# One fused Mamba-2 scan product per token tile for both directions, in a one-core Trainium2 kernel

## The reference

```python
dt = jax.nn.softplus(dt + dt_bias)             # per token, direction and head (32 heads of 64 columns)
yc_f, hc_f = ssd_chunked(x_c, dt_c[:, :, 0], a[0], b_c, c_c, h0)      # forward, context, then latent from its state
yc_b, hc_b = ssd_chunked(flip(x_c), flip(dt_c[:, :, 1]), a[1], flip(b_c), flip(c_c), h0)     # backward
...
y = (yf + flip(yb)).astype(xs.dtype) + xs * d_skip[:, None]
y = y.reshape(bb, ll, SSD_D_INNER) * jax.nn.silu(z)                    # then a norm per group, then @ w_out
```

## Time and profile before

| | |
|---|---|
| median of three runs | 1770.62 us |
| the profiled execution's own time | 1770.7 us |
| its span in the trace | 1768.9 us |
| mean granted TensorE clock | 0.979 of full |
| PE, DVE, ACT, POOL busy, share of the span | 89%, 35%, 21%, 14% |
| the scan: first and last of line 943's matmuls start | 276.3 and 490.1 us |

### The profile page before, as it was taken

The page is one execution under the profiler, slowest core; times in us unless marked ns, Lnnn a source line. Parts: engine busy times, 40 slices in busy tenths (PEclk is TensorE's granted clock), DMA queues, the critical chain, the costliest instruction groups (busy, mean ns, idle before and its releaser), DMA issues. The chain is left out here.

```text
span 1768.9 us, 22244 instructions
## 1 busy us (share of the span) xinstructions
PE 1582.5 (89%) x8812; PEld 832.7 (47%) x8812; DVE 613.4 (35%) x1294; ACT 370.6 (21%) x761; POOL 253.2 (14%) x266
## 2 busy tenths in 40 slices
PE   5999999999999979899788788798989998878887
PEld 3534445666545555455444344344555544444443
DVE  2433447778724223422111112647422211111112
ACT  2221146887710110000000000217210000000000
POOL 2001013434320010110101012111011110101001
PEclk9899999999999989999999999899989999999999
DMA  9477767999260489999999999822479999999996
GB/s 376 176 283 299 288 229 185 317 319 309 72 254 24 155 336 426 425 425 425 426 428 426 428 427 417 340 111 75 185 274 424 425 425 426 426 427 427 426 426 259
DMA packets 141922, 572.77 MB, mean 324 GB/s; under 512 B 22360, under 2 KB 79208, under 8 KB 111120
## 3 DMA queue, kind: packets, MB, share of 16 engines
q1 hardware_dynamic: 121296, 525.49, 74.2%
q0 software_dynamic: 14784, 26.11, 4.1%
q10 hardware_dynamic: 5760, 20.06, 3.5%
HBM read 543.52 MB, written 49.25 MB: 335 GB/s over the span
## 5 line engine op out<-in xcount | busy, mean ns | idle before, releaser
L1944 PE MATMUL bank<-mem 128*64 128x256 f32 x4160 | 503.1, 393 | 73.3 <-DMA mem<-in_moe_w_gate_dram 45.3
L1944 PEld LDWEIGHTS bank<-mem 128*64 128x64 f32 x4160 | 296.4, 136 | 279.2 <-issue 50.3
L1957 PE MATMUL bank<-mem 128*64 128x512 f32 x1040 | 238.3, 600 | 44.0 <-DMA mem<-in_moe_w_down_dram 38.7
L626 PE MATMUL bank<-mem 128*128 128x512 f32 x384 | 173.3, 604 | 0.9 <-DMA mem<-in_ssd_w_in_dram 0.9
L1890 POOL DMA_INDIRECT ys_dram<-mem x61 | 61.2, 1003 | 771.1 <-DVE mem L2178 700.1
L2108 ACT ACTIVATE mem<-bank 128x256 f32<-128x256 f32 x65 | 24.9, 383 | 685.0 <-PE bank L1944 685.0
L1957 PEld LDWEIGHTS bank<-mem 128*64 128x64 f32 x1040 | 70.8, 137 | 172.3 <-issue 117.2
L2178 DVE TENSOR_TENSOR mem<-bank,mem 128x512 f32<-128x512 f32 x65 | 44.9, 691 | 222.1 <-PE bank L1957 167.2
L2157 DVE TENSOR_TENSOR mem<-mem,bank 128x256 f32<-128x256 f32 x65 | 27.4, 421 | 268.3 <-PE bank L1944 135.2
L626 PEld LDWEIGHTS bank<-mem 128*128 128x128 f32 x384 | 71.9, 192 | 99.4 <-issue 97.6
L920 PE MATMUL bank<-mem 128*128 128x512 f32 x256 | 115.2, 593 | 0.0
(11 more groups left out here) (333 smaller groups left out, 1505.4 us busy)
## 6 DMA issues: line engine op xcount, KB each, us to landing
mem<-in_moe_w_up_dram SPq DMA_DIRECT2D x64, 2048.0 KB, 26.4
mem<-in_moe_w_down_dram SPq DMA_DIRECT2D x64, 2048.0 KB, 26.7
mem<-in_moe_w_gate_dram SPq DMA_DIRECT2D x63, 2048.0 KB, 26.4
mem<-in_mod_w_dram SPq DMA_DIRECT2D x24, 2048.0 KB, 9.0
ys_dram<-consts SPq DMA_DIRECT2D x55, 512.0 KB, 7.8
mem<-in_ssd_w_in_dram SPq DMA_DIRECT2D x10, 2048.0 KB, 9.3
mem<-ac_dram ACTq DMA_DIRECT2D x32, 512.0 KB, 5.6
mem<-in_ssd_w_out_dram SPq DMA_DIRECT2D x4, 2048.0 KB, 11.0
```

The costliest lines, as they stand in the source:

```text
L626: mm = nc.tensor.matmul(psum[c % 2][:, :], lhsT=w[:, k, (c % 4) * P:(c % 4 + 1) * P], rhs=aT[0][:, k, :], start=(k == 0), stop=(k == KD - 1))
L1944: mm = nc.tensor.matmul(bank[half * BR:(half + 1) * BR, 0:HF], lhsT=x[:, k], rhs=w[k][:, half::2], start=(k == 0), stop=(k == KD - 1), ski ...
L1957: mm = nc.tensor.matmul(bank[half * BR:(half + 1) * BR, :], lhsT=ht[:, k // 2, k % 2 * BR:(k % 2 + 1) * BR], rhs=w[:, k, half * COLS:(half ...
```

## The change

It does five things. dt goes out of the product: after the decays, `lndt` = ln(max(dt, 1.2e-38)) is formed (one DVE, one ACT instruction), `ltop` is its largest value over the heads, and the column term `acol` gets ltop − lndt added (three DVE instructions); the Exp of each piece gets a bias from `ltop`, so it yields decay·dt. The `xdt` multiply on POOL goes, and line 943's product reads x itself. The decay matrices are made per tile, forward then backward (`piece`, tiles 3, 2, 1, 0), in three buffers `EB`. In each odd step POOL adds the two masked matrices of a tile (128x1024), and only then PE multiplies the sum by x: eight products in odd steps, none in even ones. And DVE's tail changes: an odd step evacuates bank 5, a step from place 2 on bank 6, 16 adds instead of 20 per group.

The diff, with waits and helpers of the later stages left out:

```diff
@@ -705,6 +705,9 @@
...
         nega = region(A_WORK + 5760, 64)
+        lndt = tmp6[3]
+        ltop = small(2 * NT)
+        DT_TINY = 1.2e-38
         dtrow = region(A_Y + 2048, 512)
...
@@ -759,6 +762,7 @@
...
                                     bc(nega.rearrange("p (d h) -> p d h", d=2), 1, NT), ALU.mult).then_inc(dt_A, 1)
+            nc.vector.tensor_scalar(lndt, dtf, DT_TINY, None, ALU.max).then_inc(dt_w, 1)
         def decay_dve(dve):
...
@@ -768,6 +772,12 @@
...
                 nc.vector.tensor_tensor(wend[:, d], EX[:, d, :, 1, :], dt[:, :, d, :], ALU.mult).then_inc(wend_ok, 1)
+            dve.wait_ge(dt_l, 2)
+            ln = lndt.rearrange("p (t d h) -> p t d h", t=NT, d=2)
+            link(dve, nc.vector.tensor_reduce(ltop, lndt.rearrange("p (n h) -> p n h", h=HEADS), AX, ALU.max))
+            link(dve, nc.vector.tensor_tensor(ln, bc(ltop.rearrange("p (t d) -> p t d", t=NT), 3, HEADS), ln,
+                                              ALU.subtract))
+            nc.vector.tensor_tensor(acol, acol, ln.rearrange("p t d h -> p d t h"), ALU.add).then_inc(wend_ok, 1)
         def dt_act(act):
...
@@ -785,6 +795,8 @@
...
                                      ACT.Exp).then_inc(ex_ev, 1)
+            act.wait_ge(dt_w, 2)
+            nc.scalar.activation(lndt, lndt, ACT.Ln).then_inc(dt_l, 1)
         def decay_pe(pe):
...
@@ -803,13 +815,12 @@
...
         y = region(A_WORK, 4096, "p (b t n) -> p b t n", b=2, t=NT)
-        xdt = region(A_WORK + 4096, 1024, "p (b r n) -> p b r n", b=2, r=HG)
         xw = region(A_WORK + 5120, 1024, "p (b r n) -> p b r n", b=2, r=HG)
...
         acB = region(A_Y + 2048, 2048, "p (b r n) -> p b r n", b=2, r=HG)
-        EB = region(A_Y + 4096, 2048, "p (b r n) -> p b r n", b=2, r=HG)
+        EB = [region(at, 1024, "p (r n) -> p r n", r=HG) for at in (A_Y + 4096, A_Y + 5120, A_WORK + 4096)]
         h = region(A_Y + 6144, 1024, "p (d n) -> p d n", d=2)
...
@@ -820,14 +831,16 @@
...
         STEPS = [(0, 2), (1, 3), (0, 3), (1, 2), (0, 0), (1, 1), (0, 1), (1, 0)]
-        FIRST = (0, 1, 4, 5)
+        TILES = (3, 2, 1, 0)
+        SKIPS = {1: 3, 3: 2, 4: 0, 5: 1}
+        SKIPPED = (1, 3, 5, 5)
         SK, NH = len(STEPS), len(STEPS) - 2
...
         sc_ac = [sem(f"sc_ac{i}") for i in range(2)]
-        sc_xdt = sem("sc_xdt")
+        sc_sum = sem("sc_sum")
         sc_xw = sem("sc_xw")
...
@@ -852,35 +865,45 @@
         def heads(v, g):
...
-        def firsts(i):
+        def reads(i):
             g, k = divmod(i, SK)
-            return 4 * g + sum(f < k for f in FIRST)
+            return (SK - 1) * g + k
+        def skips(i):
+            g, k = divmod(i, SK)
+            return 4 * g + sum(f < k for f in SKIPS)
+        def piece(i):
+            k = i % SK
+            return k % 2, TILES[k // 2]
         def scan_pool(pool):
-            pool.wait_ge(wend_ok, 2)
+            pool.wait_ge(wend_ok, 3)
             pool.wait_ge(sc_in, 32)
...
                 d, t = STEPS[k]
-                b = i % 2
                 if k == 0:
                     pool.wait_ge(cv_row, 4 * (g + 1))
-                x_g = xrow[:, g, t, :].rearrange("p (r n) -> p r n", r=HG)
-                if i >= 2:
-                    pool.wait_ge(sc_y, i - 1)
-                nc.gpsimd.tensor_tensor(xdt[:, b], x_g, bc(heads(dt[:, t, d], g), 2, HD), ALU.mult).then_inc(sc_xdt, 1)
                 if k < NH:
...
                         pool.wait_ge(sc_st, n - 1)
+                    x_g = xrow[:, g, t, :].rearrange("p (r n) -> p r n", r=HG)
                     nc.gpsimd.tensor_tensor(xw[:, n % 2], x_g, bc(heads(wend[:, d, t], g), 2, HD), ALU.mult).then_inc(
                         sc_xw, 1)
-                if k in FIRST:
-                    if i >= 4:
-                        pool.wait_ge(sc_yev, i - 3)
-                    nc.gpsimd.tensor_tensor(xd[:, firsts(i) % 2], x_g, bc(heads(dskip, g), 2, HD), ALU.mult).then_inc(
-                        sc_xd, 1)
+                if k in SKIPS:
+                    n = skips(i)
+                    if n >= 2:
+                        pool.wait_ge(sc_yev, (SK - 1) * ((n - 2) // 4) + SKIPPED[(n - 2) % 4])
+                    x_g = xrow[:, g, SKIPS[k], :].rearrange("p (r n) -> p r n", r=HG)
+                    nc.gpsimd.tensor_tensor(xd[:, n % 2], x_g, bc(heads(dskip, g), 2, HD), ALU.mult).then_inc(sc_xd, 1)
+                if k % 2:
+                    pool.wait_ge(sc_mix, i + 1)
+                    nc.gpsimd.tensor_tensor(EB[i % 3], EB[i % 3], EB[(i - 1) % 3], ALU.add).then_inc(sc_sum, 1)
                 if k == 1 and g:
...
@@ -895,10 +918,10 @@
...
         def cb_pe(pe, i):
             g, k = divmod(i, SK)
-            t = STEPS[k][1]
+            t = TILES[k // 2]
             if k == 0:
                 pe.wait_ge(cv_silu, 20 + g + 1)
-            n = firsts(i)
+            n = i // 2
             if n:
...
@@ -925,24 +948,24 @@
...
                 d, t = STEPS[k]
-                b = i % 2
                 gate(i // 2, k % 2)
-                if (i + 1) % SK in FIRST and i + 1 < NI:
+                if k % 2 and i + 1 < NI:
                     cb_pe(pe, i + 1)
                 if i >= 1:
-                    pe.wait_ge(sc_yev, i)
+                    pe.wait_ge(sc_yev, reads(i - 1))
                 else:
...
                     pe.wait_ge(sc_h, NH * g + k - 1)
-                    nc.tensor.matmul(psum[6][:, :], lhsT=CT[:, g, t * P:(t + 1) * P], rhs=h[:, d, :],
-                                     start=True, stop=True)
-                pe.wait_ge(sc_mix, i + 1)
-                pe.wait_ge(sc_xdt, i + 1)
-                for r in range(HG):
-                    mm = nc.tensor.matmul(psum[5][:, r * HD:(r + 1) * HD], lhsT=EB[:, b, r, :], rhs=xdt[:, b, r, :],
+                    mm = nc.tensor.matmul(psum[6][:, :], lhsT=CT[:, g, t * P:(t + 1) * P], rhs=h[:, d, :],
                                           start=True, stop=True)
-                mm.then_inc(sc_y, 1)
+                if k % 2:
+                    pe.wait_ge(sc_sum, i // 2 + 1)
+                    for r in range(HG):
+                        mm = nc.tensor.matmul(psum[5][:, r * HD:(r + 1) * HD], lhsT=EB[i % 3][:, r, :],
+                                              rhs=xrow[:, g, TILES[k // 2], r * HD:(r + 1) * HD], start=True, stop=True)
+                if k:
+                    mm.then_inc(sc_y, 1)
                 if k < NH:
...
@@ -1008,28 +1031,33 @@
...
         def rows_act(act, i):
-            g, k = divmod(i, SK)
-            d, t = STEPS[k]
+            g = i // SK
+            d, t = piece(i)
             act.dma_start(acB[:, i % 2].rearrange("p r n -> p (r n)"),
...
         def decays_act(act, i):
-            g, k = divmod(i, SK)
-            d, t = STEPS[k]
+            g = i // SK
+            d, t = piece(i)
             b = i % 2
             act.wait_ge(sc_ac[b], 16 * (i // 2 + 1))
-            if i >= 2:
-                act.wait_ge(sc_y, i - 1)
+            if i < 3:
+                act.wait_ge(wend_ok, 3)
+            elif i % 2:
+                act.wait_ge(sc_sum, (i - 3) // 2 + 1)
+            else:
+                act.wait_ge(sc_y, reads(i - 3))
             for r in range(HG):
                 hd = g * HG + r
-                seg = nc.scalar.activation(EB[:, b, r, :], acB[:, b, r, :], ACT.Relu, scale=-1.0,
+                seg = nc.scalar.activation(EB[i % 3][:, r, :], acB[:, b, r, :], ACT.Relu, scale=-1.0,
                                            bias=acol[:, d, t, hd:hd + 1])
...
                 rows_act(act, i + 2)
-            decay = EB[:, b].rearrange("p r n -> p (r n)")
-            nc.scalar.activation(decay, decay, ACT.Exp, scale=-1.0).then_inc(sc_e, 1)
+            decay = EB[i % 3].rearrange("p r n -> p (r n)")
+            nc.scalar.activation(decay, decay, ACT.Exp, scale=-1.0, bias=ltop[:, 2 * t + d:2 * t + d + 1]).then_inc(
+                sc_e, 1)
         def scan_act(act):
             def silu(n):
@@ -1047,7 +1075,7 @@
...
             def evac(i):
                 g = i // 4
-                act.wait_ge(sc_xdt, SK * (g + 1))
+                act.wait_ge(sc_y, (SK - 1) * (g + 1))
                 act.wait_ge(sc_xw, NH * (g + 1))
...
@@ -1073,9 +1101,8 @@
...
         def masks_dve(dve, i):
-            k = i % SK
-            n = firsts(i)
-            tb = STEPS[k][1] % 2
+            n = i // 2
+            tb = piece(i)[1] % 2
             dve.wait_ge(sc_cb, n + 1)
...
@@ -1085,40 +1112,41 @@
...
         def mix_dve(dve, i):
-            d, t = STEPS[i % SK]
-            b = i % 2
-            if i % SK in FIRST:
+            d, t = piece(i)
+            if i % 2 == 0:
                 masks_dve(dve, i)
             dve.wait_ge(sc_e, i + 1)
-            nc.vector.tensor_tensor(EB[:, b], EB[:, b], bc(cbm[:, t % 2, d, :], 1, HG), ALU.mult).then_inc(
-                sc_mix, 1)
+            nc.vector.tensor_tensor(EB[i % 3], EB[i % 3], bc(cbm[:, t % 2, d, :], 1, HG), ALU.mult).then_inc(sc_mix, 1)
```

(37 more changed lines are left out.)

4 lines of the change are left out of this document (2 added, 2 removed).

## The result

The kernel after takes 1762.39 us (median of six runs, 1760.16 to 1763.44), the kernel before 1772.4 in the six runs beside it (1767.99 to 1774.13): ratio 0.9942, 95% interval 0.9928 to 0.9957, 10 us less. The forecast was 1758.0 with a range up to 1764, and faster at 0.90. So the time is inside the range, but the loss is not where the forecast saw it.

What follows compares the result with a forecast made beforehand. The scan was taken as PE-bound, with ACT close behind. 8.8 us saved before group 3, minus 3.0 for the clock, plus 6.9 in group 3 gave 12.7 us off 1770.7: forecast 1758.0 us, range 1747 to 1764.

Steps and rivals of the forecast that it cites:

- PE will stand in front of group 3's first gate some 8 to 12 us: Scan: PE waits for the fourth z unit's load; savings of groups 0 to 2 beyond 8.8 us are lost.
- the chain through the add: Scan: DVE tail, mask product, POOL add take 5.8 us, at worst 7.9, hidden in PE's 9.95 us.
- Zeros and landing: SP's queue: zero writes take 3.9 us longer; fourth z unit issued at 413.4, landing 13.6 later at 427.0.
- The clock: After PE's gap before group 3: about 6 us at granted clock 0.50, 3.0 us of work lost, bounds 0 and 4.
- Group 3 saves 6.9: Scan's last group: four batches fewer, first gate to last products 45.8 us instead of 52.7; bounds 4.9 and 7.4.
- Rival B: Scan: DVE and POOL slow each other, the add delays PE, 8 us of the sum lost, 1766 us; chance 0.16.
- Exp: ACT in the scan: bias from memory adds 0.1 us to each Exp of 1.06, 3.0 us over 30.
- add: POOL in odd steps: the 128x1024 add takes 2.5 us, at worst 4.0, and stays hidden from PE.
- preparation: After the decays: the Ln chain, under 4 us, hides in ACT's 8.59 us idle; cost 0, 4 us at most uncovered.
- downstream: After the scan: everything up to the experts' weight stream hangs on PE and passes the shift on; cost 0.
- A: Group 3's start: fourth z unit no obstacle, scan ends 21.9 us sooner by ACT's limit, 1748 us; chance 0.14.
- D: Behind the scan: savings waited for again on a fixed-time load; gain under 3.5 us, 1769 us; chance 0.07.

Runs made afterwards that it cites:

- the odd tails first: Kernel after, with DVE doing an odd step's tail before the next mask product instead of after it: 1763.25 us, ratio 0.9927 to the kernel before.
- the dt run: Kernel before with only dt moved into the exponent, no dt multiply on POOL, still two products per tile, no add: 1775.94 us, ratio 1.0005.

## Why the prediction was right or wrong

**The clear gain, and its size: right.** The sum gave 12.7 us less against its profiled execution; 10 were measured. That the size agrees is luck: one loss was in it that did not come, and another was missing.

**PE bounds the scan, 27.7 us the most it can give back: right.** In the kernel after every stretch but one ran at PE's pace.

**"PE will stand in front of group 3's first gate some 8 to 12 us": wrong, the step that failed.** The wait was 0, which the forecast itself had named as a sign of being wrong. It rested on PE, or ACT, running at their limits through groups 0 to 2, and that in turn on "DVE: 16 adds fewer in the tails, none on the path: gain 0" and "in that time DVE ends its tail (three instructions of 0.69, 2.1 us)". DVE's tail ahead of place 3's evacuation is not 2.1 us: with the held addition, the norm's 2.45 us, the masks and the mask product it is 10.5 (338.33 to 348.83), and 5.1 of it lie behind the end of place 3's products at 343.7. The forecast counted the chain through the add and left out the second chain, from products through evacuation and state update to PE's next bank. The jams held PE back by some 9 us in groups 1 and 2, and with 2.9 in group 0 it came to group 3 at 426.92, behind the unit's 422.5. The limit itself was there: with less of the jam PE met it, for 1.2 us with the add on DVE, 1.6 with the norm cut, and 3.1 with the odd tails first, there with a clock of 0.50.

**Zeros and landing: a size off.** 2.3 us longer instead of 3.9; landing after 11.3 us instead of 13.6; 422.5 instead of 427.0. Even at 427.0 PE, at the gate at 426.92, would hardly have waited. With the odd tails first the unit did land at 427.1.

**The clock: right in kind, other place.** 3.0 us were taken for one gap; 3.4 us were lost behind two jams. Its reading that the trace of the kernel before shows 0.50 only behind a gap such as the 4.34 us one is wrong: eleven stretches of 3.4 to 10.2 us at 0.50 lie in it, all outside the scan, the one from 76 us on behind a gap of 1.1 us, the one from 619 behind gaps of 0.4 and 0.7. The rule of the Trainium skill that the forecast set aside (TensorE: Matmul & The Clock Gate, "HAM oscillation — how this bites in real kernels") is borne out in part. Its price, half of the throttled time, agrees (3.4 us at 0.50, 1.7 lost), and with the odd tails first the clock fell in a wait for a transfer. But it fell behind waits for DVE too, of 1.3 and 1.9 us, in groups 1 and 3 and not in group 2; and in the version with the norm behind place 4 it fell behind one single gap of 1.8 us, before group 3's first products, and not behind its twin before group 2's.

**Group 3 saves 6.9: wrong.** From first gate to last products it took 478.28 - 426.92 = 51.4 us, against 52.7, a gain of 1.3. It had its own jam of 5.6, and the last products began at 478.3 instead of at 475 to 476.

**Rival B, "DVE and POOL disturb each other": this is what happened in the mechanism, elsewhere than said.** It was priced on the chain through POOL's add in group 3; it fell on the addition to y in all groups, and needed the norm beside it. Its time, 1766, was 3.6 us above the median measured, the forecast's 4.4 below. The Trainium skill (GPSIMD Engine Reference, section 1) has GpSimd's SBUF interfaces shared with VectorE for instructions with two SBUF inputs; the trace agrees: of the tail's instructions, the ones with two such inputs were held (2.35 instead of 0.69 us), those that read PSUM were not (0.68 to 0.69).

**Exp, add, preparation, downstream: right.** 1.15, 2.35, nothing (the dt run), and a shift that is passed on.

**Rivals A and D.** The unit was no obstacle, as A says, because PE came later than thought; but A's price, ACT's limit and 1748 us, did not come with it. D did not happen: nothing behind the scan is seen to take the gain.
